# Retention heads: the same 96 dense pieces, put behind 11 of the 22 small products instead of behind all of them

## What is computed

```
s     = einsum(q, k) * dmask                 # decay mask within the chunk
inner = einsum(s, v)
cross = einsum(q, r_state) * q_dec           # from the chunks before
r_new = gamma**length * r_state + einsum(k * k_dec, v)
o     = (inner + cross) * rsqrt(mean(o*o) + eps) * silu(gate)
```

## Time and profile before

| | us |
|---|---|
| median of 3 runs | 5916.66 (5916.29 to 5924.08) |
| the profiled execution | 5915.66 |
| its span, first to last instruction | 5913.9 |
| TensorE busy with matmuls | 5771.2 |
| VectorE busy | 3824.7 |
| ScalarE busy | 2289.4 |
| DMA, mean over the span | 115 GB/s |

### The profile page before, as it was taken

The page is one execution under the profiler, slowest core; times in us unless marked ns, Lnnn a source line. Parts: engine busy times, 40 slices in busy tenths (PEclk is TensorE's granted clock), DMA queues, the critical chain, the costliest instruction groups (busy, mean ns, idle before and its releaser), DMA issues. The chain is left out here.

```text
span 5913.9 us, 112816 instructions
## 1 busy us (share of the span) xinstructions
PE 5771.2 (98%) x48599; PEld 5619.0 (95%) x48599; DVE 3824.7 (65%) x4811; ACT 2289.4 (39%) x2840; POOL 489.0 (8%) x324
## 2 busy tenths in 40 slices
PE   7999999999999999989999999999999999999999
PEld 7888889999999999989999999999999999999998
DVE  5565652323237643256876678777777888888998
ACT  3333331222223332122234444333335556556555
POOL 0000000000000000000016661111110000000000
PEclk9999999999999999999999999999999999999999
DMA  3111112222223443321324445554545433435542
GB/s 102 37 51 39 49 40 103 108 87 108 86 90 131 156 130 131 115 86 59 107 100 158 160 165 153 150 149 142 155 129 182 147 106 114 147 111 149 169 128 84
DMA packets 374407, 682.04 MB, mean 115 GB/s; under 512 B 219616, under 2 KB 234976, under 8 KB 346464
## 3 DMA queue, kind: packets, MB, share of 16 engines
q1 hardware_dynamic: 366928, 656.81, 33.5%
q10 hardware_dynamic: 7056, 19.00, 0.8%
HBM read 562.37 MB, written 113.37 MB: 114 GB/s over the span
## 5 line engine op out<-in xcount | busy, mean ns | idle before, releaser
L2724 PE MATMUL ps<-va_h_high,va_v_high 128*128 128x288 f32 x3584 | 1056.3, 295 | 10.3 <-DVE va_h_low L140 7.6
L2726 PE MATMUL ps<-va_h_high,va_v_low 128*128 128x288 f32 x3584 | 1057.7, 295 | 0.0
L2725 PE MATMUL ps<-va_h_low,va_v_high 128*128 128x288 f32 x3584 | 1056.5, 295 | 0.0
L2724 PEld LDWEIGHTS ps<-va_h_high,va_v_high 128*128 128x128 f32 x3584 | 673.4, 188 | 11.1 <-DVE va_v_low L140 7.8
L2726 PEld LDWEIGHTS ps<-va_h_high,va_v_low 128*128 128x128 f32 x3584 | 673.4, 188 | 0.0
L2725 PEld LDWEIGHTS ps<-va_h_low,va_v_high 128*128 128x128 f32 x3584 | 673.3, 188 | 0.0
L140 DVE TENSOR_TENSOR ah_ul<-ah_u,ah_uh 128x1024 fp32r<-128x1024 f32 (+1 forms) x288 | 435.1, 1511 | 212.8 <-ACT ah_uh L2278 160.5
L1145 PE MATMUL ps<-rwkv_hn_high,rwkv_wh 128*128 128x288 f32 x1664 | 492.9, 311 | 7.0 <-PEq L225 7.0
L140 DVE TENSOR_TENSOR rwkv_wl<-ret_w,rwkv_wh 128x2048 fp32r<-128x2048 f32 (+1 forms) x138 | 260.7, 1890 | 369.2 <-ACT rwkv_wh L1246 304.5
L1146 PE MATMUL ps<-hn_low,rwkv_wh 128*128 128x288 f32 x1664 | 470.5, 298 | 0.0
L2104 PE MATMUL ps<-hn_high,ah_uh 128*128 128x288 f32 x1536 | 431.9, 297 | 5.0 <-DVE ah_ul L140 4.8
(11 more groups left out here) (488 smaller groups left out, 14839.0 us busy)
## 6 DMA issues: line engine op xcount, KB each, us to landing
va_v<-peer_v SPq DMA_DIRECT2D x96, 1024.0 KB, 5.5
ah_u<-peer_u SPq DMA_DIRECT2D x160, 512.0 KB, 6.3
ah_u<-peer_u SPq DMA_DIRECT2D x48, 1024.0 KB, 5.1
ret_w<-w_ret SPq DMA_DIRECT2D x47, 1024.0 KB, 4.8
h_kept<-ah_h SPq DMA_DIRECT2D x128, 288.0 KB, 2.3
gates<-ah_stage SPq DMA_DIRECT2D x12, 3072.0 KB, 9.7
ah_hidden<-h_kept SPq DMA_DIRECT2D x60, 576.0 KB, 4.9
ah_v<-peer_v SPq DMA_DIRECT2D x30, 1024.0 KB, 4.9
```

The source lines that it names most:

```text
L2724: pe.matmul(z, ah[:, r, f], th[:, q, r, :], start=begin, stop=False, skip_group_check=True)
L2725: pe.matmul(z, ah[:, r, f], tl[:, q, r, :], start=False, stop=False, skip_group_check=True)
L2726: done = pe.matmul(z, al[:, r, f], th[:, q, r, :], start=False, stop=r == R - 1, skip_group_check=True)
```

## The change

The pieces of a head are put behind other points. `fill_of` now has 0 at swq, s0, s2, o0 to o4, RS0, RS1 and RS3; 9 at swk, 6 at t2, 7 at s1, s3 and R0 to R3, 5 at s4, and 14 at RS2 and ss; 6 stay at the head's start. It is 96 as before. By this table 11 of the 22 small products have pieces behind them. Nothing else changes.

```diff
@@ -1046,13 +1046,13 @@
-        fill_of = {"lead": 6, "swq": 3, "swk": 6, "t2": 5}
-        fill_of.update({f"s{c}": 4 for c in range(NT)})
+        fill_of = {"lead": 6, "swq": 0, "swk": 9, "t2": 6}
+        fill_of.update({"s0": 0, "s1": 7, "s2": 0, "s3": 7, "s4": 5})
         for c in range(NRC):
-            fill_of.update({f"o{c}": 3, f"R{c}": 4})
-        fill_of[f"o{NRC}"] = 4
-        fill_of.update({f"RS{p}": 4 for p in range(4)})
-        fill_of["ss"] = 8
+            fill_of.update({f"o{c}": 0, f"R{c}": 7})
+        fill_of[f"o{NRC}"] = 0
+        fill_of.update({"RS0": 0, "RS1": 0, "RS2": 14, "RS3": 0})
+        fill_of["ss"] = 14
         points = list(fill_of)
```

## The result

| | before | changed |
|---|---|---|
| median, us | 5917.16 (6 runs, 5916.29 to 5924.08) | 5939.12 (6 runs, 5935.35 to 5941.59) |
| the profiled execution, us | 5915.66 | 5938.94 |
| retention stage in its trace, us | 852.7 | 875.1 |
| windows of the eight heads at clock 0.50, in stretches of 3.41 us | 11 | 29 |

The ratio is 1.0035, 95% interval 1.0022 to 1.0048: slower by 22 us, more than the 0.2% that can be told from no change. The forecast was 5912.7 us in a range up to 5926.

A forecast was written before the change was run, and what follows sets the result against it. TensorE's own instructions were taken to bound the stage. From the median 5916.66 us, 7.2 us saved at RS seams and 3.2 us lost to the clock gave 5912.7 us, no difference, range 5903 to 5926.

The forecast's parts named there:

- What bounds the kernel: Retention stage: only TensorE's own instructions hold it; eight heads take about 794 us, 13% of the span.
- Seams with 128 rows cost nothing: Swaps, s and o products beside dense pieces: closing these seams changes 0 us, at most 1.1 us up or down.
- Seams of RS: 7.2 us saved: RS0 to RS2 in a row drop two of three 0.41 us charges: 0.90 us per head, bounds 0 to 13.1.
- the pitches forecast for two and three stretches: Head repeat time in the changed profile: 99.3 us with two stretches at clock 0.50, 100.9 with three.
- Rival 2: RS row: each RS still pays for uncovered first loads, so only 3.2 us are saved: 5916.7 us; chance 0.08.
- The clock: 13 stretches, two more than now: At and behind o4: 13 stretches at half clock instead of 11, costing 3.2 us; bounds 8 to 24 stretches.
- Rival 1: RS row behind o4: 64-row products don't bring the clock back; 16 to 24 stretches, likeliest 20, 5923.8 us; chance 0.24.
- Rival 3: At o0: a wait for s4 if its 0.8 us of spare cover fails, +12 us, 5924.7 us; chance 0.06.
- Rival 4: All closed seams: switching costs more than the rows show and clock stays up; 5881 or 5899 us; chance 0.09.
- The rule on batches: Skill advice favouring long dense stretches; the prediction held that runs of four already keep 2.4 GHz, so longer ones win nothing.

The follow-up runs named there:

- e1: Changed kernel with the old table from o4 on (4 pieces behind o4 and each RS, 8 at ss): 5913.66 us, ratio to before 0.9990.
- e6: Against e3, o4 in quarters: two pieces behind each of the first three, one behind the last: 5893.85 us, ratio to before 0.9964.
- e4: Changed kernel with the RS products made over 128 rows, the lower 64 zeros: 5908.24 us, ratio to before 0.9982.
- e8: e6 with the RS products made over 128 rows, the lower 64 zeros: 5883.32 us, ratio to before 0.9943.
- e11: Kernel before, own table, with the RS products made over 128 rows, the lower 64 zeros: 5907.99 us, ratio to before 0.9984.
- e10: Changed kernel with the swap of q made twice, 0.97 us more work per head: 5935.49 us, ratio to before 1.0030.
- e3: Changed kernel with 7 of RS2's 14 pieces moved behind o4: 5915.55 us, ratio to before 0.9996.
- e5: Against e3, 4 of o4's 7 pieces put between its two halves, 3 behind it: 5913.27 us, ratio to before 0.9991.

## Why the prediction was wrong, point by point

- **What bounds the kernel.** Right. TensorE's own instructions fill the stage before and after, and nothing else came in.
- **Seams with 128 rows cost nothing.** Right within what can be seen: the pitch without lowered clock went from 97.04 us to 96.13 (96.17 from the heads 102.49 apart), 0.9 us, which the RS seams explain alone; e1, which closes only seams of the other kind but keeps the old tail, has the pitch of before less 0.1 (98.5 against 98.6 with one stretch), 0.9 us in eight heads against a bound of 1.1.
- **Seams of RS: 7.2 us saved.** Right: 7 us, and the pitches forecast for two and three stretches came true. (One reading was off without weight: the change of rows inside o4, taken as 0.09 us, is nearer 0.14, since the two short records take 0.36 us and those of 8 columns are 0.11 apart.) The charge lies at the change between dense pieces and 64 rows; a row of three pays it once (e6), and 128 rows never (e4, e8, e11). Rival 2, the first loads of each RS staying uncovered, is out: in e6 the row of three RS costs 0.40 us over its columns, as one RS alone did, not three times that or near it.
- **The clock: 13 stretches, two more than now.** This is the step that failed. The mechanism was named and bounded (8 to 24 stretches), the value taken was that of dense pieces: "RS streams its columns nearly without a gap, so it is nearer to the dense pieces than to o4". What the runs showed in its place is 29: RS with 64 rows at half speed did not bring the clock back in any head of this order, and the same row with 128 rows does (e4: 15). Of the 18 stretches more, 7 go by e10 to the pitch at which the heads repeated, and 11 to this. The upper bound of three stretches per head was too low as well, because at half speed o4's rest and the row together last up to 9 us (1636.02 to 1644.95), and dense work then needs some 4.7 us more.
- **Rival 1** was what happened. It had 0.24 and 5923.8 us, and the range stopped at 5926. At 29 stretches its own price is 5916.7 - 7.2 + 18 x 1.59 = 5938 us, one from the measured 5939.1. What it lacked was the pitch: I let the heads differ, while from head 2 on each met the same case. A head with four stretches takes 102.45 us, and the falls then lie 102.4 apart, so the next head met nearly the same case; e10, whose heads are 0.97 us longer, broke the row.
- **Rival 3**, a wait of o0 for s4: no wait appeared, the 0.8 us held. **Rival 4**: the switch costs no more than the rows showed.
- **The rule on batches**, that matmuls should run back to back because the engine's power follows its use (the Trainium skill, "Perfetto Trace Analysis", "Matmul Optimizations"): the changed kernel has longer batches than before and a lower mean clock (0.94 against 0.98 from 1000 to 1700 us), though TensorE has no idle time there in either. The runs show the other side of making them: what is taken out from between thin products leaves those in a row. e6 does the reverse, splits the thin part with batches of two pieces, and is the faster for it.

## What to carry to other kernels

Where TensorE is the bound, look for its thin parts (few columns, or half of the rows idle) before the number of changes between kinds of work: here a seam cost 0.4 us at 64 rows and nothing at 128, a lowered clock 1.6 us for each 3.41 us. Spread dense work through the thin part in small portions, as e6 does, rather than behind it, and count what comes directly behind a thin part as a part of it if it can't bring the clock back. And where a loop repeats, take the number of lowered stretches per round as something that can repeat exactly: it is then worth a run, not a mean.

## What the runs showed that was not expected

- Products over 64 rows with all their columns, twelve records in a row, did not raise the clock again in 5.4 us, where the same records over 128 rows did. The 64 rows more were zeros. So zeros that only fill up rows paid twice here: some 0.4 us for each charge, and the lowered clock.
- Entered at full clock, with dense pieces before and behind it, the same row of three RS over 64 rows (2.8 us) did not lower it (e3, e6).
- Adding 7.8 us of work did not make the changed kernel slower: its stage went from 875.1 to 872.0 us (e10).
- Two halves of 2.2 us with 3.2 us of dense work between them each brought falls of their own in six heads of eight (e5); quarters of 1.1 us with 1.6 us between them none (e6).
